# Attention of a hybrid encoder step: a plain query layout, heads in halves of the PE array, three steps in flight

## What is computed

```python
q, k, v = jnp.split(h @ w_qkv, 3, axis=-1)          # 16 heads of 64
# per chunk c of 64 queries: the keys of its own chunk and of the 8 chunks before it (576 keys)
s = einsum('bqhd,bkhd->bhqk', q_c, k_c) * scale + bias   # bias: learned, clipped relative position
s = where(valid, s, NEG);  p = softmax(s)
o = einsum('bhqk,bkhd->bqhd', p, v_c)
x = x + o @ w_o
# the 32 sample rows do the same over 256 cached keys and their own 32
```

## Time and profile before

| | us |
|---|---|
| median of 3 runs (range) | 2694.64 (2694.21 to 2696.08) |
| the profiled execution's own time | 2693.13 |
| its span, first to last instruction | 2691.4 |
| PE busy in the span | 2592.8 (96%) |
| first pair's scores begin, at | 70.8 |
| pair 3, its stretch of the span (333.5 to 420) | 86.5 |
| Wo of pair 7 ends, first FFN begins, at | 769.5 |

### The profile page before, as it was taken

How to read it: one execution, slowest core, us unless ns; L and a number is a source line. 1 busy time by engine, 2 the same in 40 slices (tenths; PEclk the granted TensorE clock), 3 DMA queues, 4 the chain that set the end, 5 groups by cost and what they waited for, 6 DMA issues and landing times.

```text
span 2691.4 us, 43514 instructions
## 1 busy us (share of the span) xinstructions
PE 2592.8 (96%) x15759; PEld 2509.1 (93%) x15759; DVE 1604.1 (60%) x3274; ACT 898.7 (33%) x1703; POOL 240.0 (9%) x553
## 2 busy tenths in 40 slices
PE   7999999999689999999999999999999999999998
PEld 7888888888579999999999999999899999999998
DVE  5566656665566666666666643342766666666666
ACT  4433343334353222222222542132522222222223
POOL 1000000000030000000000231122100000000003
PEclk9999999999899999999999999999999999999999
DMA  6111111110001111111111020111111111111111
GB/s 156 33 33 37 36 33 33 40 37 21 16 32 48 41 38 47 47 47 47 47 47 47 32 69 28 32 49 63 47 48 47 39 39 47 46 35 44 47 47 74
DMA packets 100272, 120.57 MB, mean 45 GB/s; under 512 B 3676, under 2 KB 88836, under 8 KB 100164
## 3 DMA queue, kind: packets, MB, share of 16 engines
q1 hardware_dynamic: 96644, 109.12, 12.7%
q0 software_dynamic: 2864, 7.88, 1.2%
q10 hardware_dynamic: 656, 2.12, 0.2%
HBM read 108.70 MB, written 10.40 MB: 44 GB/s over the span
## 4 chain that ended last, share of the span: by engine, by line
PE 88%; DVE 4%; ACT 3%; POOL 2%; issue 2%; DMA 0%; ACTq 0%; DVEq 0%; POOLq 0%
PE psum L157 25%; PE psum L159 25%; PE psum L158 25%; PE psum L845 4%; PE psum L884 2%; POOL total L228 2%; PE psum L829 2%; PE psum L881 1%; PE psum L1666 1%; DVE x L1121 1%; DVE gx_lo L216 1%; PE psum L770 0%; ACT conv_t L1350 0%; ACT v L781 0%; DVE gx_lo L1825 0%
## 5 line engine op out<-in xcount | busy, mean ns | idle before, releaser
L157 PE MATMUL psum<-gx_hi,w_hi 128*128 128x352 f32 x3264 | 1073.3, 329 | 17.1 <-DVE gx_lo L216 7.0
L158 PE MATMUL psum<-gx_lo,w_hi 128*128 128x352 f32 x3264 | 1058.4, 324 | 0.0
L159 PE MATMUL psum<-gx_hi,w_lo 128*128 128x352 f32 x3264 | 1057.8, 324 | 0.0
L157 PEld LDWEIGHTS psum<-gx_hi,w_hi 128*128 128x128 f32 x3264 | 617.6, 189 | 23.9 <-issue 15.3
L158 PEld LDWEIGHTS psum<-gx_lo,w_hi 128*128 128x128 f32 x3264 | 617.8, 189 | 2.3 <-issue 0.7
L159 PEld LDWEIGHTS psum<-gx_hi,w_lo 128*128 128x128 f32 x3264 | 617.5, 189 | 0.0
L1442 DVE TENSOR_TENSOR x<-x,psum 128x352 f32<-128x352 f32 x528 | 258.9, 516 | 122.4 <-PE psum L159 122.4
L1350 ACT ACTIVATE conv_t<-a_gate,cur 128x352 f32<-128x352 f32 x132 | 90.2, 683 | 534.7 <-DVE a_gate L1407 534.5
L157 PE MATMUL psum<-h_hiA,w_hi 128*128 128x352 f32 x528 | 172.3, 326 | 4.3 <-DVE x L1442 4.3
L157 PE MATMUL psum<-h_hiB,w_hi 128*128 128x352 f32 x528 | 172.5, 327 | 0.0
L159 PE MATMUL psum<-h_hiB,w_lo 128*128 128x352 f32 x528 | 171.9, 326 | 0.0
(11 more groups left out here) (181 smaller groups left out, 3410.2 us busy)
## 6 DMA issues: line engine op xcount, KB each, us to landing
raw<-in_f_w_up SPq DMA_DIRECT2D x44, 1024.0 KB, 5.1
raw<-in_f_w_down SPq DMA_DIRECT2D x22, 1024.0 KB, 4.9
raw<-in_a_w_qkv SPq DMA_DIRECT2D x24, 512.0 KB, 3.9
raw<-in_b_w_in SPq DMA_DIRECT2D x8, 1024.0 KB, 5.5
raw<-in_a_w_o SPq DMA_DIRECT2D x8, 512.0 KB, 3.4
raw<-in_b_w_out SPq DMA_DIRECT2D x4, 1024.0 KB, 4.9
out<-raw SPq DMA_DIRECT2D x6, 512.0 KB, 2.7
xin<-in_x_prompt SPq DMA_DIRECT2D x4, 512.0 KB, 8.3
```

The lines of the kernel that those rows point to most:

```text
L157: pe.matmul(out, w[0], rhs[0], start=first, stop=False)
L158: pe.matmul(out, w[0], rhs[1], start=False, stop=False)
L159: return pe.matmul(out, w[1], rhs[0], start=False, stop=last)
```

## The change

Only the attention is rewritten, on all engines.

- Queries lie plainly (`q_tok`, 128 partitions by 1024 + 128 positions). A step takes 128 queries of one head at once over a window of up to 640 keys (five blocks); head 0 uses array rows 0 to 63, head 1 rows 64 to 127. Keys outside a chunk's band are masked: by -1e30 in the bias tile, and in steps 4 to 7 by a DVE memset on PSUM.
- PV takes, for each head, the 64 columns of its values as stationary and 128 moving columns; head 0's result goes to PSUM partitions 0 to 63, head 1's to 64 to 127, in bank 6.
- Three steps are in flight: scores of s, turning of s-1, PV of s-2. The third group of transposes of a step stands inside the linear tile.
- DVE handles both heads in one instruction for the bias, the maximum and the inverse.
- The bias is loaded per pair, two DMAs on SP ahead of the pair's weights, behind a wait until all scores of the pair before have been biased.
- Wo's first 12 tiles stand around the turning of the last step; the next pair waits for 22 of the 24 adds.
- Pair 6 leaves its Wo to pair 7, which does it between its own steps (four tiles a step in steps 0 to 3, two in steps 4 to 7), and pair 7 writes `o` to tensors of its own.
- The clearing of `p_even` and `qd` goes; POOL clears the bias corners once.

The core of the diff (the loop of the PE, the scores, PV, and DVE's maxima):

```diff
-                    stat = qd[par][:, 2 * s + odd, :]
...
-                        for i in range(2):
-                            last = pe.matmul(psum[:, 2 * odd + i, :n // 2], stat,
-                                             kT[par][:, first + i * n // 2:first + (i + 1) * n // 2],
-                                             start=True, stop=True)
+        def scores(t, par, s):
+            if s:
+                pe.wait_ge(exp_done, 2 * STEPS * t + 2 * s)
...
+                for i in range(parts):
+                    for h in range(2):
+                        mm = pe.matmul(psum[:, 2 * h + i, :m], q_tok[par][HEAD_ROWS[h], P * s:P * (s + 1)],
+                                       kT[par][HEAD_ROWS[h], first + m * i:first + m * (i + 1)], start=True, stop=True)
...
+        def weigh(t, par, s):
...
+                    for h in range(2):
...
+                            v = v_tok[par][:rows, kb if s < NB else NB, HEAD_ROWS[h]]
+                        mm = pe.matmul(psum[HEAD_ROWS[h], 6, :m], v, pT[:rows, g, P * (2 * i + h):P * (2 * i + h) + m],
+                                       start=(kb == blocks[0]), stop=(kb == blocks[-1]))
...
+            for s in range(STEPS + 2):
+                if s < STEPS:
+                    scores(t, par, s)
+                    if late and s < 4:
+                        late_wo(t, s, 0)
+                if s >= 2:
+                    weigh(t, par, s - 2)
+                if s == STEPS and not (at_pair(t, LAST - 1)):
+                    wo_tiles(t, 0, KT)
+                if 1 <= s <= STEPS:
+                    turn(t, s - 1, range(min(2, len(key_groups(s - 1)))))
+                if s == STEPS and not (at_pair(t, LAST - 1)):
+                    wo_tiles(t, KT, EARLY_WO)
...
+                    linear(pe, out, w_hi[slot], w_lo[slot], c, None, range(KT // 2))
+                    turn(t, s - 1, third)
+                    linear(pe, out, w_hi[slot], w_lo[slot], c, None, range(KT // 2, KT)).then_inc(qkv_done, 1)
...
+                part, b = psum[:, 1:4:2, n // 2 - 2 * P:n // 2], bias[:, par, :, :]
...
+            dve.tensor_tensor(part, part, b, ALU.add).then_inc(biased, 1)
+            if masked(s):
+                dve.memset(psum[HEAD_ROWS[1], 0:4:2, :CK], NEG).then_inc(biased, 1)
+            dve.wait_ge(biased, 1 + B_PAIR * t + biases_to(s + 1))
+            dve.tensor_reduce(neg_max[:rows_of(s), :], both_scores(s), AX.XY if n > BANK else AX.X, ALU.max,
+                              negate=True).then_inc(max_done, 1)
```

And SP's part:

```diff
         def pair(t, par, units):
+
+            sp.wait_ge(biased, 1 + B_PAIR * t)
+            stand(sp)
+            load_bias(sp, t + 1, 1 - par)
             for k in units:
```

More of the change, by code:

```diff
@@ L159, in product, with linear @@
         return pe.matmul(out, w[1], rhs[0], start=False, stop=last)
-    def linear(pe, out, hi, lo, c, norm=None):
-        for k in range(KT):
+    def linear(pe, out, hi, lo, c, norm=None, tiles=range(KT)):
+        for k in tiles:
             if norm is not None:
@@ L389, in input_sp @@
         sp.wait_ge(first_sq, NB + 1)
[L390 to L392 removed]
+        load_bias(sp, 0, 0)
     def input_act_dma(act):
@@ L602, in build @@
[L602 to L644, removed]
+    GROUP_BANK = [4, 5, 4]
+    def groups_to(s):
+        return sum(len(key_groups(j)) for j in range(s))
@@ L922, in attention_pe @@
[L922 to L939 removed]
+                    extra_pe(pe, e, 1 - par, 6)
@@ new lines, in exps @@
+        def exps(t, s):
+            m, n = rows_of(s), window(s)[1]
+            for h in range(2):
+                if h == 0:
+                    act.wait_ge(max_done, STEPS * t + s + 1)
+                dst = probs[s % 2][h][:m, :n]
+                if n > BANK:
+                    dst = dst.rearrange("p (i n) -> p i n", i=2)
+                act.activation(dst, scores_of(s, h), ACT.Exp, bias=neg_max[:m, h:h + 1],
+                               accum_out=row_sum[:m, h:h + 1]).then_inc(exp_done, 1)
@@ new lines, in pair @@
+        def pair(t, par):
+            base = KV_FIRST + KV_PAIR * t
+            late = at_pair(t, LAST)
+            for s in range(STEPS + 2):
+                if s == 0 and late:
+                    act.wait_ge(qkv_done, STEPS * PAIRS)
+                    Unit(LAST, LAST_PAR, 0).act(act)
+                if s >= 2:
+                    start, n = BLOCKS[s - 2]
+                    act.wait_ge(pv_done, 2 * (STEPS * t + s - 1))
+                    act.activation((O_LAST if late else O_MAIN)[0][:, start:start + n], psum[:, 6, :n], ACT.Copy)\
+                        .then_inc(o_hi_done, 1)
+                if s == STEPS and not late and not (at_pair(t, LAST - 1)):
+                    act.wait_ge(qkv_done, STEPS * (t + 1) + 9)
+                    Unit(t, par, 4).act(act)
+                if 1 <= s <= STEPS:
+                    copy(t, s - 1, range(min(2, len(key_groups(s - 1)))))
+                if s < STEPS:
+                    exps(t, s)
+                if 1 <= s <= STEPS and len(key_groups(s - 1)) > 2:
+                    copy(t, s - 1, [2])
+                if s == 0 and not late:
@@ L997, in pair @@
-                for e in extras(s, True, following):
-                    n = plan.extra[s, e]
-                    act.wait_ge(t_done, base + n + 1)
-                    if e == ("v", 0, 1, 2, 3):
+                    Unit(t, par, 1).act(act)
+                elif s in (3, 6) and not late:
+                    act.wait_ge(qkv_done, STEPS * (t + 1) + s)
+                    Unit(t, par, s // 3 + 1).act(act)
+                if s in EXTRAS and (not late or s == 2):
+                    act.wait_ge(kv_turned, base + extras_to(s) + 1)
+                    if s == 3:
@@ L1135, in build @@
+        with dve.Fori(0, PAIRS // 2 - 1) as j:
+            pair(2 * j, 0)
+            pair(2 * j + 1, 1)
+        pair(LAST - 1, 0)
+        pair(LAST, LAST_PAR)
+        ffn[0].split(None, dve, 0, 0)
+        for n in range(EARLY_WO, BURST):
+            norm.dve_tile(dve, *divmod(n, KT))
     DOWN = NCH * KT
```

646 lines of the change are left out of this document (313 added, 333 removed).

## The result

The changed kernel takes 2596.48 us, the median of four runs (2593.85 to 2599.97); the kernel before took 2694.43 on the same chip. The ratio is 0.9638, with a 95% interval of 0.9621 to 0.9655. A second series of five runs beside later experiments gave 2596.39 (0.963, 0.9616 to 0.9643). The profiled execution took 2593.85, with a span of 2592.3.

A forecast was written before the change was run, and what follows sets the result against it. The PE's own work bounds pairs 0 to 6, waiting on its chain pair 7. Terms: -31 for six pairs, -4 pair 6, -20 pair 7, -3 behind: -58 on 2693.1, 2636 us; range 2588 to 2690.

The forecast's parts named there:

- The signs listed: Trace marks of a right forecast: overlapping score pairs 0.27 us apart, step about 8, pair 7 near 60, sums about 31.
- the overlap: Scores and PV of two heads in array halves, partly side by side: -2.7 and -5.6 us a pair.
- the rule of M + 1 slots: Scores and PV: a head's 2M records beside the other's need M + 1 slots, as only second and first overlap.
- their lower ends: Scores and PV wholly side by side: 6.95 and 6.5 us a pair; rival with free changes too, 2579, chance 0.17.
- The changes of the array: About 29 shape changes a pair at 0.15 us: +4.35 (0 to +7.8); rival at 0.27 each, 2664, chance 0.15.
- The ends of a pair: Waits at a pair's end, in Wo and the sample's PV: -1.2 us a pair (-2.5 to +1.0).
- The 0.61 and the 0.63: Pair's end: next scores' wait for the last add and sample PV's for ACT's copy, in us; first goes, second covered.
- the 1.27: Pair's end: the fifth Wo tile's wait in us for the first add; it stays, as DVE still splits weights first.
- Pair 7: Last pair, from pair 6's last linear tile to the last PV: 83.4 us falls to 63.3, so -20.
- Behind it: From the last PV to the end of POOL's sums: 34.5 us falls to about 31.5, -3 (0 to -5).
- late next: Behind pair 7: DVE's split, moved behind the adds, comes late by 1.2 us, under POOL's sums.
- The new wait in the step: Rival: ACT's copies ahead of the exponentials delay the step; decides only beyond 1.6 us more a step; no separate chance.

The follow-up runs named there:

- e2: The changed kernel with turning and PV alternating by key group, adding 16 changes of the array's division a pair and no work: 2620.0 us, ratio 0.9719.
- e8: The changed kernel with DVE's split of the next pair's first weights put behind Wo's first four adds in pairs 0 to 5: 2587.85 us, ratio 0.96.
- e4: The changed kernel, but pair 6 does its own Wo at its end and pair 7 has no late Wo: 2606.93 us, ratio 0.968.
- e5: The changed kernel with DVE's first FFN weight split put back ahead of the 21st add of pair 7: 2600.17 us, ratio 0.9641.
- e1: The changed kernel with all of head 0 before head 1 in scores and PV, same instructions: 2628.51 us, ratio 0.9751.
- e7: The changed kernel with head 0's four PV records ahead of head 1's inside each group of two key blocks: 2596.41 us, ratio 0.9638.
- e10: The changed kernel with early FFN split and norm tiles, Wo's first four adds ahead of the split, and the loop written out: 2575.39 us, ratio 0.9555.

## Why the prediction was right, and which terms were off

**The bound, the direction and the mechanism** were right: the PE set the time of pairs 0 to 6, the halves do work at once, changes of the array give part of it back, and the PE still sets the pace (97%). The signs listed came: paired starts 0.27 us apart, a step of about 8 us, pair 7 near 60, POOL's sums some 31 behind the last PV.

**The term that was mis-sized is the overlap.** The step that failed is the rule of M + 1 slots, taken "because the halves share neither rows nor PSUM banks, while a record needs the end of the one before it in its half". It lets the records start in program order, where both of head 0's records stand ahead of head 1's first. They do not: one half takes 0.27 us from record to record, so two that start 7 ns apart are of different heads, and head 1's first (263.119) is ahead of head 0's second (263.485). The first half of the reason was no condition either: PV's halves share all 128 rows and bank 6, and overlap as fully as the scores. So the records run in pairs, and the streams shrink to their lower ends, 6.95 us of scores and 6.5 of PV: -5.2 and -6.4 a pair in place of -2.7 and -5.6. That is 3.3 us a pair, some 23 of the 40 us over seven pairs. The rule of the Trainium skill that stood against it, in "TensorE: Matmul & The Clock Gate", Part 3, was the better guide on this point: the trace agrees with it on the span of packed tiles, with 7 ns between the heads where it gives about 4 for each further tile.

**The changes of the array** were forecast at 0.15 each, 4.35 a pair, and cost a little more. From the starts in a middle pair (456.43 to 532.45), beside the pace inside a group, a change from the whole array to row halves takes 0.20 us (0.09 ahead of the first score record and 0.10 behind it), from row to column halves 0.15, from column halves to the whole array 0.16. There are 29 in a pair, as counted, some 4.9 us. e2 gives 0.16 for the last kind and its way back. The bracket's ends, 0 and 0.27, are both out. What the Trainium skill says in "TensorEngine Tiling (Array Packing)", Tiling Modes, of a drain is borne out as a price of 0.15 to 0.20 us.

**The ends of a pair** were taken at -1.2. The 0.61 and the 0.63 did go; the 1.27 stayed as 1.12, as said, and e8 shows that it was the split. Not counted were the turning's other losses. Before, 63 transposes at 0.109 are 6.9 of its 9.26 us; besides the 0.63 there are two waits of about 0.25 for a copy of V, as this one in the timeline of before, and restarts behind waits:

```profile
281.55 0.33 PE L829 MATMUL psum<-ident,p_even 128*128 128x128 f32 x1 [0.25 <-ACT v L781]
```

After, 66 transposes are 7.2 of 7.90, and half a microsecond of the rest is changes. So some 1.5 us a pair went that no term had, 10 of the 40 us, by these rows; no run tests it by itself. The prediction had put a price only on the waits with a name at the pair's end. The overlap and this are some 33 of the 40 us; the rest is in small pieces that the runs do not part.

**Pair 7** came out at 63.3 as forecast, and stage by stage within 1 us: closing pair 6 took 3.8 for 4.2, steps 0 to 3 20.9 for 20, steps 4 to 7 25.1 for 25.6, step 8 5.0 for 4.3, the end 8.5 for 9.2. That the errors cancel to a tenth is luck. The larger overlap did not matter there, as DVE and the chain set the pace; the wait of 2.81 us (step 4's scores behind a late add) is DVE coming last in step 3 (it is busy for 1.87 of the 2 us from 615), which the forecast of 20 had in its total. The clock fell for a moment only (0.97 for the stretch), and e4 shows that without the late Wo it falls further. **Behind it** 31.1 for 31.5, and the split that is "late next" lies under POOL's sums, as said; e5 shows that it costs nothing.

**The new wait in the step** did not come in the middle pairs: DVE's maximum over 1280 values takes 1.49, as worked out. Without filler it does show, in e4's 12.4 us, there with a lower clock as well.

## What to carry to other kernels

Matmuls in two halves of the PE array ran fully side by side here when their instructions alternated, and almost so with four records of one half ahead of the other's (0.05 us a step); a float32 matmul counts as two. Set against the gain 0.15 to 0.20 us for each change of the array's shape, and group the work to make few of them. Where a trace names a wait, ask what else ends there before removing it: 6.3 us under POOL's sums were worth nothing, 1.1 us at the PE in each of six pairs were worth 8.6 in all. And ask what the filler does for the clock: taking work out of pair 7 left it as long as it was.

## What the hardware showed that was not expected

- One half of the array takes four records; a fifth holds up the other half's records behind it. That is read from e1's starts (0.71 us lost a step with ten in turn) and borne out by e7 (0.05 with four).
- Records of different halves do not start in program order: in e1 head 1's first starts at 438.263, ahead of head 0's eighth at 438.366, though it stands behind the tenth. "TensorE: Matmul & The Clock Gate", Part 3, in the Trainium skill says that matmuls start strictly in order; across the halves of this trace they don't, and the measurement decides.
- A linear matmul starts 0.03 us behind the last of a group of transposes (266.454 and 266.482), where a further transpose starts after 0.109. It is no gain: the matmul behind it comes 0.246 later in place of 0.16, so that the two steps together are 0.27 either way. A table of times from start to start puts that time into the wrong row.
- A turn of the loop costs 2.4 to 3.1 us of idle time here, with no releaser named, and up to 2.5 more in the pair behind it, where matmuls run in part at 1.2 GHz. Written out (e10), both go. What the engine does in that idle time the runs don't show.
